# Head rounds: every eviction of a projection unit placed ahead of the attention work of its slot on ScalarE

## The chip, the cores and the metric

One Trainium2 chip, one core. The metric is the device time in microseconds of one execution of the whole layer; the numbers given for a kernel are its median over several executions. Profiled times come from one further execution, taken by the hardware profiler.

## The reference, cut to what matters

One decoder layer on x of 1 x 1024 x 1024, all in float32:

```python
proj = rms_norm(x) @ w_in            # q, k, v of 8 attention heads; q, k, v, i, f, o of 8 mLSTM heads; gates
oa = diff_attention(q, k, v)         # per head: softmax(q0 k0) - lam * softmax(q1 k1), causal, times v
hm = mlstm_chunkwise(qm, km, vm, i, f)
ya, yb = rms(oa) @ w_proj_a, (sigmoid(ml_o) * rms(hm)) @ w_proj_b
h = x + (g0 * ya + g1 * yb) @ w_out
h = h + relu(rms_norm(h) @ w_ff1) ** 2 @ w_ff2
out = rms_norm(h)
```

## The kernel before

Everything is written by hand: each engine has its own instruction stream, and semaphores order the streams.

The input projection is cut into blocks of 128 output columns, and each block into two halves of 512 positions. One half is a *unit*: 24 matmuls of 128x512 (three split products for each of 8 slices of the contraction, L716 to L718) into one of two PSUM banks, `gp[0]` for even units and `gp[1]` for odd ones. A head needs 6 blocks, so 12 units, numbered 0 to 11. ScalarE evicts a unit with `evac` (L1059 to L1064): it waits until the *previous* contents of the SBUF buffer `ev[0]` or `ev[1]` are stored (`st`), then until the matmuls are done, copies 128x512 (L1062) and signals SyncE, which stores the buffer to DRAM (`proj_d`, L400). TensorE may start unit k+2 only when unit k is evicted.

The projection of head h runs interleaved with the attention of head h-1. This is a *head round*: rounds 1 to 7 are run by `head_round(h, h - 1)` on each engine. A round has 16 slots. The table `QUARTERS` says how many quarter units TensorE computes in each slot, (4, 4, 5, 0, 3, 2, 3, 3, 4, 4, 4, 4, 2, 2, 4, 0), and `ENDS_AT[s]` lists the units that end in slot s. No slot ends more than one: units 0, 1 and 2 end in slots 0, 1 and 2, unit 3 in slot 4, units 4 to 9 in slots 6 to 11, units 10 and 11 in slots 13 and 14. In each slot TensorE first does its quarters and then `attend(att, s)`, the attention work.

The slots that matter below, on ScalarE (`attend`, L1157):

- Slot 0: it copies the rotated k four times (`ka`, `kb`, L1166 to L1170), then q twice (L1166, L1167), then v (`vs`, L1161).
- Slot 2: it copies the transposed mLSTM v (`v1`, shown as `v` at L1178, done when TensorE has transposed it, L785), and loads the Exp table with a small activation (`warm`, L1180).
- Slots 3 to 10: the softmax exponentials of query block s-3 (`pr`, L1207), two passes. VectorE makes from them the combined attention row (`at`, L1611), which TensorE transposes in the next slot, after its quarters (L871); ScalarE copies the transposed row (`ath`, L1186), VectorE makes its low part (`atl`, L1583), and only behind that, in VectorE's order, come the maxima of the next block's scores.
- Slots 5 and 6: additionally four exponentials of 128x128 each over a row that is broadcast from DRAM (`qraw` from `u_d`, L1215).
- Slots 5 to 12: a copy of the accumulated output (`otmp`, L1195) ahead of the `ath` copy.

SyncE issues its DMAs in a written order, one queue. At the start of a round it issues: the stores of the last round's units, the loads of the attention's k, q and v, a weight block, `ckq` and `osig` (512 KB each, L438 and L440), the store of unit 0, the store of unit 1, a weight block, the two broadcast rows (L449), the store of unit 2, the store of unit 3, and so on.

In ScalarE's `head_round` the eviction of a slot's unit stands behind the slot's attention work; in slot 0 it stands between the four k copies and the two q copies. The gate round that follows round 7 has its own loop with the same form.

Of the kernel before, what the change touches and what calls it, by code (L numbers as in the profile page):

```python
# [44 lines left out]
HB = 6  # L45
# [38 lines left out]
def part_slots(quarters):  # L84

    at = [s for s, n in enumerate(quarters) for _ in range(n)]
    starts = [[k for k in range(2 * HB) if at[4 * k] == s] for s in range(SLOTS)]
    ends = [[k for k in range(2 * HB) if at[4 * k + 3] == s] for s in range(SLOTS)]
    return at, starts, ends


QUARTER_AT, STARTS_AT, ENDS_AT = part_slots(QUARTERS)
# [6 lines left out]
def wait(eng, sem, value):  # L99

    if isinstance(value, int) and value <= 0:
        return
    eng.wait_ge(sem, value)
# [27 lines left out]
def build(nc, x, positions, norm_mix_w, w_in, ml_gate_b, conv_w, conv_b, da_lambda, da_subln_w,  # L131
# [14 lines left out]
    with ExitStack() as ctx:  # L146
# [905 lines left out]
        def _(act):  # L1052
# [6 lines left out]
            def evac(n, half):  # L1059
                wait(act, st[half], 16 * n)  # L1060
                act.wait_ge(gemm_done, 2 * n + half + 1)
                act.activation(ev[half][:], gp[half][:], ACT.Copy).then_inc(gp_free, 1)  # L1062
                act.wait_ge(gp_free, 2 * n + half + 1)
                act.sem_inc(ev_ready[half], 1)  # L1064
# [76 lines left out]
            def units_of_round(h, k):  # L1141
                if k % 2 == 0:
                    b = k // 2
                    split_hi(h * HB + b + 1, h * (HB // 2) + (b + 1) // 2, (b + 1) % 2)

            def kq_wait(h, b):
                if b + 1 == 3:
                    act.wait_ge(w_loaded_q, 16 * h + 16)
# [99 lines left out]
            def head_round(h, att):  # L1248
                for s in range(SLOTS):
                    for k in STARTS_AT[s]:  # L1250
                        if k % 2 == 0:
                            kq_wait(h, k // 2)
                            units_of_round(h, k)
                    for k in ENDS_AT[s][:-1]:
                        evac(h * HB + k // 2, k % 2)

                    def evac_units():
                        for k in ENDS_AT[s][-1:]:
                            evac(h * HB + k // 2, k % 2)

                    attend(att, s, evac_units)
                    if s:
                        evac_units()

            head_round(1, 0)
            with act.Fori(2, NH) as h:
                head_round(h, h - 1)
# [27 lines left out]
            for j in range(2 * KT):  # L1295
# [7 lines left out]
                else:  # L1303
                    for i in range(2):
                        k = j - KT
# [800 lines left out]
```

## Time and profile before

| | |
|---|---|
| median of 3 runs | 2007.83 us (2005.05 to 2009.06) |
| profiled execution: time, span | 2009.17 us, 2007.4 us |
| TensorE busy | 96% of the span |
| VectorE, ScalarE, GpSimd busy | 59%, 48%, 18% |
| rounds 1 to 7 | about 130 to 870 us of the span |
| evictions L1062 in the whole kernel | 128, 591 ns each |
| stores of evictions | 128, 256 KB each |

Rows of the profile give the start in us from the start of the span, the duration in us, then engine, line and operation with output and inputs. A bracket at the end holds the idle time of the engine just before it and what ended it. For a DMA the landing time is the time from its issue until all its data are there.

### The profile page before, as it was taken

The numbers are of one execution on the slowest core, as the hardware profiler recorded it, in microseconds if no ns is written. First come the engines' busy times: TensorE is split into PE (matmuls) and PEld (weight loads), VectorE is DVE, ScalarE is ACT, GpSimd is POOL, SyncE is SP. The second block draws the span as 40 slices with busy tenths as digits, with TensorE's granted clock in tenths as the row PEclk, the third lists the DMA queues.
The fourth block names the chain that finished last, engine by engine and source line by source line (L and its number), as shares of the span: only waits on it lengthen the run. The fifth ranks groups of instructions, "written<-read, shape, count | busy, mean of one in ns | idle before, by whom it ended". The sixth has DMA issues, their size and how long they took to land. (4 is left out here: it accounts for less than half of the span.)

```text
span 2007.4 us, 26057 instructions
## 1 busy us (share of the span) xinstructions
PE 1923.8 (96%) x9378; PEld 1605.9 (80%) x9378; DVE 1180.8 (59%) x1537; ACT 966.1 (48%) x1634; POOL 364.8 (18%) x204
## 2 busy tenths in 40 slices
PE   5989999999999999999998999999999999999998
PEld 4768888788888787878886888888888888888886
DVE  5736666566575757543321112278677787888874
ACT  4346565556465555544433333225765765533341
POOL 1211211212111121211121444441000000021002
PEclk9989999999999999999999999999999999999999
DMA  5562657645544546273435443645686785563422
GB/s 150 88 153 66 148 84 131 99 120 107 123 104 110 120 72 158 59 176 70 68 88 162 155 150 104 224 157 210 220 289 210 255 281 196 210 237 132 163 82 84
DMA packets 207825, 291.79 MB, mean 145 GB/s; under 512 B 36840, under 2 KB 127592, under 8 KB 200832
## 3 DMA queue, kind: packets, MB, share of 16 engines
q1 hardware_dynamic: 195520, 281.98, 50.9%
q10 hardware_dynamic: 12224, 8.72, 1.3%
q8 instruction: 52, 0.85, 0.2%
q14 instruction: 29, 0.24, 0.0%
HBM read 203.56 MB, written 87.10 MB: 145 GB/s over the span
## 5 line engine op out<-in xcount | busy, mean ns | idle before, releaser
L716 PE MATMUL gp<-r1h,w_hi 128*128 128x512 f32 x1152 | 457.4, 397 | 13.9 <-ACT ev L1062 12.3
L718 PE MATMUL gp<-r1h,w_lo 128*128 128x512 f32 x1152 | 452.1, 392 | 0.0
L717 PE MATMUL gp<-r1l,w_hi 128*128 128x512 f32 x1152 | 451.6, 392 | 0.0
L1967 POOL TENSOR_TENSOR w_lo<-w_raw,w_hi 128x1024 fp32r<-128x1024 f32 x88 | 219.2, 2491 | 896.8 <-ACT w_hi L1057 896.8
L716 PEld LDWEIGHTS gp<-r1h,w_hi 128*128 128x128 f32 x1152 | 218.2, 189 | 59.7 <-issue 8.1
L718 PEld LDWEIGHTS gp<-r1h,w_lo 128*128 128x128 f32 x1152 | 217.8, 189 | 46.6
L717 PEld LDWEIGHTS gp<-r1l,w_hi 128*128 128x128 f32 x1152 | 218.3, 189 | 42.3
L977 PE MATMUL scores<-xh,qh 128*128 128x512 f32 x512 | 200.1, 391 | 1.4 <-ACT res L1367 1.3
L981 PE MATMUL scores<-xh,ql 128*128 128x512 f32 x512 | 199.3, 389 | 0.0
L979 PE MATMUL scores<-xl,qh 128*128 128x512 f32 x512 | 199.2, 389 | 0.0
L1207 ACT ACTIVATE pr<-scores,nb 128x256 f32<-128x256 f32 (+7 forms) x128 | 93.9, 739 | 122.2 <-DVE nb L1601 120.6
L1779 DVE TENSOR_TENSOR xl<-xraw,xh 128x2048 fp32r<-128x2048 f32 x54 | 127.8, 2367 | 0.0
L1062 ACT ACTIVATE ev<-gp 128x512 f32<-128x512 f32 x128 | 75.6, 591 | 87.9 <-PE gp L718 49.4
L1321 ACT ACTIVATE qh<-rq 128x2048 fp32r<-128x2048 f32 x32 | 61.2, 1914 | 114.8 <-DVE rq L1808 73.8
L1057 ACT ACTIVATE w_hi<-w_raw 128x1024 fp32r<-128x1024 f32 x88 | 93.2, 1059 | 47.8 <-PE gp L718 20.4
L977 PEld LDWEIGHTS scores<-xh,qh 128*128 128x128 f32 x512 | 96.1, 188 | 23.5 <-ACT res L1367 3.0
L1599 DVE TENSOR_REDUCE mx<-scores 128x1 f32<-128x256 f32 (+7 forms) x128 | 91.4, 750 | 38.6 <-PE scores L811 38.1
L981 PEld LDWEIGHTS scores<-xh,ql 128*128 128x128 f32 x512 | 96.1, 188 | 20.1
L979 PEld LDWEIGHTS scores<-xl,qh 128*128 128x128 f32 x512 | 96.1, 188 | 20.0 <-issue 0.2
L1333 ACT ACTIVATE xh<-xraw 128x2048 fp32r<-128x2048 f32 x54 | 102.8, 1904 | 9.2 <-DMA xraw<-xo_d 9.2
L716 PE MATMUL gp<-r2h,w_hi 128*128 128x512 f32 x256 | 102.1, 399 | 3.5 <-issue 3.5
L1783 DVE TENSOR_TENSOR ql<-rq,qh 128x2048 fp32r<-128x2048 f32 x32 | 76.6, 2392 | 46.4 <-ACT qh L1321 46.4
(340 smaller groups left out, 3650.8 us busy)
## 6 DMA issues: line engine op xcount, KB each, us to landing
xraw<-xo_d SPq DMA_DIRECT2D x54, 1024.0 KB, 5.1
proj_d<-ev SPq DMA_DIRECT2D x128, 256.0 KB, 3.2
rq<-in_w_ff SPq DMA_DIRECT2D x32, 1024.0 KB, 7.8
w_raw<-in_w_in SPq DMA_DIRECT2D x56, 512.0 KB, 9.2
xo_d<-res SPq DMA_DIRECT2D x78, 256.0 KB, 3.2
xo_d<-ring SPq DMA_DIRECT2D x60, 256.0 KB, 2.9
pr<-proj_d SPq DMA_DIRECT2D x16, 512.0 KB, 5.6
gt<-proj_d SPq DMA_DIRECT2D x32, 256.0 KB, 2.7
```

Source lines behind the costliest of these rows:

```text
L716: pe.matmul(gp[half][:], wh[slot][:, k, :], mh[:, k, t], start=(k == 0), stop=False)
L717: pe.matmul(gp[half][:], wh[slot][:, k, :], ml[:, k, t], start=False, stop=False)
L718: mm = pe.matmul(gp[half][:], wl[slot][:, k, :], mh[:, k, t], start=False, stop=(k == KT - 1))
L977: pe.matmul(bank, qh[s % 3][:, k, cols], xh[s % 3][:, k, :], start=first and k == 0, stop=False, skip_group_check=True)
L979: pe.matmul(bank, qh[s % 3][:, k, cols], xl[s % 3][:, k, :], start=False, stop=False, skip_group_check=True)
L981: mm = pe.matmul(bank, ql[s % 3][:, k, cols], xh[s % 3][:, k, :], start=False, stop=(k == UN - 1), skip_group_check=True)
L1057: act.activation(wh[slot][:], raw[slot][:], ACT.Copy).then_inc(w_hi, 1)
L1207: act.activation(pr[:, c, 0:(i + 1) * P], sp_[:, c, 0:(i + 1) * P], ACT.Exp, bias=nb[:, c:c + 1], scale=SCALE, accum_out=rs[:, i, c:c + 1] ...
L1333: act.activation(xh[s % 3][:], xraw[(s + 1) % 2][:], ACT.Copy).then_inc(p_hi, 1)
L1599: m = dve.tensor_reduce(mx[:, c:c + 1], sp_[:, c, 0:(i + 1) * P], AX_X, ALU.max)
L1779: dve.tensor_tensor(xl[s % 3][:], xraw[(s + 1) % 2][:], xh[s % 3][:].bitcast(F32), ALU.subtract).then_inc(p_lo, 1)
L1967: pool.tensor_tensor(wl[slot][:], raw[slot][:], wh[slot][:].bitcast(F32), ALU.subtract).then_inc(w_split, 1)
```

## The change

The eviction of the unit that ends in a slot is moved, on ScalarE, from behind `attend(att, s)` to in front of it, in all slots of rounds 1 to 7. In slot 0 it moves from between the k copies and the q copies to ahead of the k copies. Nothing is added or removed; no other engine's stream is edited, and the gate round keeps its form.

```diff
-                    for k in ENDS_AT[s][:-1]:
+                    for k in ENDS_AT[s]:
                         evac(h * HB + k // 2, k % 2)
-
-                    def evac_units():
-                        for k in ENDS_AT[s][-1:]:
-                            evac(h * HB + k // 2, k % 2)
-
-                    attend(att, s, evac_units)
-                    if s:
-                        evac_units()
+                    attend(att, s, lambda: None)
```

## Rows read from the trace of the kernel before

**Rows 1.** Waits of TensorE, 140 to 1000 us: what waited, total us, times, longest

```profile
PE tr L871 <- DVE at L1611: 7.2, 3, 2.8
PE gp L716 <- ACT ev L1062: 6.9, 3, 3.5
PE tr L905 <- DVE nd L1682: 6.2, 7, 0.9
```

**Rows 2.** Timeline of ScalarE in round 5, slots 0 to 4

```profile
554.12 1.06 ACT L1166 ACTIVATE ka<-kraw 64x1024 fp32r<-64x1024 f32 x1 [3.66 <-DVE kraw L1570]
...
558.34 0.58 ACT L1062 ACTIVATE ev<-gp 128x512 f32<-128x512 f32 x1
...
567.29 0.60 ACT L1178 ACTIVATE v<-tr 128x512 f32<-128x512 f32 x1 [1.93 <-PE tr L785]
...
568.40 1.28 ACT L1180 ACT_TABLE_LOAD   x1
...
569.80 0.58 ACT L1062 ACTIVATE ev<-gp 128x512 f32<-128x512 f32 x1
570.63 0.37 ACT L1207 ACTIVATE pr<-scores,nb 128x128 f32<-128x128 f32 x1 [0.25 <-ACT ev L1062]
...
572.83 0.28 ACT L1186 ACTIVATE ath<-tr 128x128 fp32r<-128x128 f32 x1 [1.39 <-PE tr L871]
```

**Rows 3.** Timeline of TensorE in round 5: attention work of slots 2, 4, 5

```profile
566.60 0.66 PE L785 MATMUL tr<-ident,pr 128*128 128x128 f32 x4 [0.51 <-DVE vs L1578]
...
572.46 0.33 PE L871 MATMUL tr<-ident,at 128*128 128x128 f32 x1
...
576.57 0.44 PE L871 MATMUL tr<-ident,at 128*128 128x128 f32 x2
```

**Rows 4.** Timeline of VectorE in round 5, slot 4

```profile
576.03 0.48 DVE L1611 SCALAR_TENSOR_TENSOR at<-pr,cc 128x256 f32<-128x256 f32 x1
```

**Rows 5.** Timeline of SyncE in round 5: issue, us that it took

```profile
556.76 0.34 SPq L440 DMA_DIRECT2D osig<-proj_d  x1
559.12 1.48 SPq L400 DMA_DIRECT2D proj_d<-ev  x1
```

**Rows 6.** Landing of these two DMAs, last column, us from issue

```profile
osig<-proj_d SPq DMA_DIRECT2D x1, 512.0 KB, 10.0
proj_d<-ev SPq DMA_DIRECT2D x1, 256.0 KB, 8.3
```

**Rows 7.** Round 6: timeline of ScalarE, slots 2 and 3

```profile
676.40 0.60 ACT L1062 ACTIVATE ev<-gp 128x512 f32<-128x512 f32 x1 [2.11 <-DMA proj_d<-ev]
677.25 0.37 ACT L1207 ACTIVATE pr<-scores,nb 128x128 f32<-128x128 f32 x1 [0.25 <-ACT ev L1062]
```

**Rows 8.** Round 6: timeline of TensorE, slot 4

```profile
679.08 0.33 PE L871 MATMUL tr<-ident,at 128*128 128x128 f32 x1 [2.16 <-DVE at L1611]
```

**Rows 9.** Round 2: issues of SyncE

```profile
240.54 1.67 SPq L440 DMA_DIRECT2D osig<-proj_d  x1
242.40 2.14 SPq L400 DMA_DIRECT2D proj_d<-ev  x1
```

**Rows 10.** Round 2: eviction of unit 2, ScalarE

```profile
251.24 0.58 ACT L1062 ACTIVATE ev<-gp 128x512 f32<-128x512 f32 x1
```

**Rows 11.** Round 3: ScalarE in slot 5, exponentials over the broadcast row

```profile
371.74 1.29 ACT L1215 ACTIVATE qraw<-qraw,hk 128x128 f32<-128x128 f32 x4 [3.91 <-DMA qraw<-u_d]
```

**Rows 12.** Round 3: issues of the stores of units 2 and 3, SyncE

```profile
358.88 6.92 SPq L400 DMA_DIRECT2D proj_d<-ev  x2
```

**Rows 13.** Round 3: landing of the first of them

```profile
proj_d<-ev SPq DMA_DIRECT2D x1, 256.0 KB, 14.8
```

**Rows 14.** Round 4: ScalarE in slot 5, exponentials over the broadcast row

```profile
477.75 1.29 ACT L1215 ACTIVATE qraw<-qraw,hk 128x128 f32<-128x128 f32 x4 [1.20 <-DMA qraw<-u_d]
```

**Rows 15.** Round 4: issue of the store of unit 2, SyncE

```profile
466.84 3.56 SPq L400 DMA_DIRECT2D proj_d<-ev  x1
```

**Rows 16.** Round 4: landing of that store

```profile
proj_d<-ev SPq DMA_DIRECT2D x1, 256.0 KB, 12.8
```

## Prediction

> **What bounds the kernel now.** TensorE is busy for 96% of the span, so a change on ScalarE counts only where TensorE waits for what ScalarE delivers. I read the waits of TensorE over the head rounds first, then the timelines of ScalarE, TensorE, VectorE and SyncE through slots 0 to 7, then the landing times of the stores. The waits [rows 1] show two things. Waiting for an eviction (`gp` for `ev`) costs 6.9 us in three places; all three lie after 890 us, in the gate round, whose code stays as it is. In rounds 1 to 7 TensorE never waits over 0.25 us for an eviction, so there is nothing to win by evicting earlier. What it does wait for is the attention chain: `tr` for `at` 7.2 us in three places, in rounds 3, 6 and 7, and `tr` for `nd` 0.9 us in each of seven rounds.
>
> The chain has no slack in slots 2 to 4. In round 5 ScalarE copies v at 567.29, loads the Exp table, evicts unit 2 at 569.80 and starts the first exponential at 570.63 [rows 2]. VectorE's row and TensorE's transposition of it follow; that starts at 572.46, 1.83 after the exponential, just as the quarters of slot 4 run out [rows 3]. Round 6 shows what a delay does: there the eviction of unit 2 waits 2.11 us for DMA, namely for the store of unit 0 that used the same buffer; the exponential starts at 677.25 [rows 7], the transposition at 679.08, again 1.83 later, and TensorE has waited 2.16 us [rows 8]. A late exponential is paid by TensorE one for one.
>
> **The change part by part.** 128x512 evictions stay 84 in number in these rounds, at 0.58 to 0.61 us. Only their order to other work changes, so each is priced by what it now stands before.
>
> *Slots 0 and 1.* Unit 0 ends at about 553, and ScalarE then idles until the rotated k at 554.12, with 3.66 us of idle before it [rows 2]: the eviction fits there, free. Behind the k copies it was free too, since the q copies wait for VectorE. Unit 1 has no attention work in its slot. Cost 0. If k came before the unit's end, up to 0.6 would be paid, but I see no such round.
>
> *Slot 2, the term that decides.* The eviction of unit 2 now stands before the v copies, the table load and the first exponential. Its wait for the store of unit 0 moves along. Before, a late store was covered by 2.5 us of copies and table load (567.29 to 569.80) [rows 2]. Now this work is queued behind the wait. After the store lands, the chain is: eviction 0.6, hand-over 0.2 to 0.3, then from the start of the v copies to the end of `warm` 2.6, so the exponential starts 3.4 to 3.5 after landing; before, it started 0.85 after landing, or at 570.63 if that was later.
>
> Does the store land earlier? The eviction of unit 0 ends some 5 us earlier, but SyncE issues the store behind `osig`, at 559.12 now, and is free only at 557.1 [rows 5]. `osig` lands at 556.76 + 10.0 = 566.8, the store at 559.12 + 8.3 = 567.4 [rows 5, 6], that is 0.6 behind it: it waits for the data queued before. I take the same landing; the other bound is 2 us earlier in round 5. In round 2 SyncE is busy with `osig` until 242.2 and stores at 242.40 [rows 9], so there is no earlier issue at all; its store also takes 8.3 (one row stands for both, [rows 6]) and lands at 250.7.
>
> The Trainium skill (DMA: Bandwidth & Descriptors, Queues, rings and completion order) states that on each DMA engine descriptors are consumed in ring order. The landings of `osig` and the store, 0.6 apart where the issues are 2.4 apart, agree with it; by it the earlier issue gains nothing.
>
> With these landings, round by round for the first exponential:
> - Round 5: eviction 567.4, exponential about 570.8 to 570.9 for 570.63: +0.2.
> - Round 2: 250.7 + 3.45 = 254.15. Before, the eviction was at 251.24 [rows 10] and the exponential 0.84 behind it: +2.1.
> - Round 6: landing 676.35, exponential 679.85 for 677.25 [rows 7]: +2.5. Round 7 repeats this pattern (one of the three waits of [rows 1]): +2.5.
> - Rounds 1 and 4: the store is there before unit 2 is done; the exponential comes 0.7 earlier, which gains nothing since TensorE had no wait there.
> - Round 3: about +2.4 here, but see slot 6.
>
> *Slot 4.* The eviction of unit 3, done when the quarters of slot 4 end, comes before the copy of the transposed row (`ath`, 572.83 [rows 2]). ScalarE is free at that point, so the eviction starts about 572.6 and the copy about 573.4: +0.5. Behind it in VectorE's order are the low part and the maxima of block 1; the row of block 1 (`at`, 576.03 + 0.48 [rows 4]) ends just before TensorE transposes it at 576.57 [rows 3]. So +0.5 in rounds where slot 2 brought no delay (1, 4, 5); where it did, the eviction runs while ScalarE waits, cost 0. Bounds: 0 (if the copy is covered) to 0.8 in all seven.
>
> *Slot 6.* The eviction of unit 4 comes before the output copy and the `ath` copy of block 2. By itself it costs about 0.1 at the next transposition. But it waits for the store of unit 2, which SyncE issues behind the broadcast rows. In round 3: issue 358.88, landing 14.8, so 373.7 [rows 12, 13], while ScalarE was done with the exponentials of slot 5 at 371.74 + 1.29 = 373.0, having waited 3.91 for the broadcast row [rows 11]. So the copies move from 372.9 to 374.5: +1.6. The broadcast row lands at a time set by DMA, so the +2.4 of slot 2 is swallowed by that 3.91 us wait: round 3 in all +1.6. In round 4: landing 466.84 + 12.8 = 479.6 [rows 15, 16] against 477.75 + 1.29 = 479.0 [rows 14]: +1.3, which contains its 0.5 of slot 4. In the other rounds the store is there.
>
> *Slots 7 to 14.* From slot 7 to 11 ScalarE runs behind TensorE, each slot ends one unit, and between two attention parts there stands one eviction before and after the change; cost 0. In slots 13 and 14 it waits for TensorE and VectorE anyway; the 0.9 us for `nd` [rows 1] stay. If that cover is gone, one eviction a round would be paid, 7 x 0.6 = 4.2.
>
> Sum: round 1 0.5, round 2 2.1, round 3 1.6, round 4 1.3, round 5 0.6 (0.2 + 0.5, rounded down), rounds 6 and 7 2.5 each: 11.1 us. The profiled execution took 2009.17, so 2020.3. It is 1.3 above the median of the runs shown; that gives 2019.
>
> **Rivals.**
>
> *Nothing measurable.* The stores land soon enough that no eviction waits. For it: each round's late landing is chance of the moment, and in round 5 it is a matter of tenths. Then the two waits of rounds 6 and 7 go too (-2.2 each), and slot 4 costs 0.5 in seven rounds: -0.9, so 2007. The Trainium skill (DMA: Bandwidth & Descriptors, Anatomy of one DMA) fits a DMA as about 2.0 us plus bytes over 436 GB/s, given for the GpSimd path; for 256 KB that is an estimate of 2.6 us and would give this rival. Against it: 8.3 to 14.8 measured here for exactly these stores.
>
> *Faster.* The store of unit 0, evicted 5 us earlier, gets ahead in the DMA queues, lands over 4 us sooner, so that the waits of rounds 6 and 7 vanish (-4.4), and slot 4 is covered: the 0.7 us earlier first exponential gives VectorE its convolution step earlier. 2007.8 - 4.4 = 2003.4. It decides from a landing before the v transposition ends (567.25 in round 5). Against it: SyncE's written order and the wait behind `osig`.
>
> *Slower by half.* The store lands by as much earlier as it is issued earlier (2 us in round 5, 1 in rounds 6 and 7), and the slot-4 and slot-6 costs are partly covered: rounds 6 and 7 1.5 each, round 2 2.1, rounds 3 and 4 1 each: about 7, 2014.5.
>
> *Much slower.* The eviction also holds up slots 7 to 11, and each round stalls once more: 11.1 + 4.2, 2023.
>
> **How the numbers follow.** Chances: forecast 0.40, slower by half 0.22, much slower 0.12, nothing measurable 0.16, faster 0.10. A change under 0.2%, 4 us, can't be told from none here. Of the "slower by half" and forecast cases a part of 0.02 falls within 4 us. So slower 0.72, same 0.18, faster 0.10. Range: from the no-change case, 2006.5, to a little over "much slower", 2024.
>
> **What would show it.** In the profile of the changed kernel, evictions L1062 with a DMA store as releaser in several of rounds 2 to 7, ahead of the v copies, and the table load L1180 behind them; TensorE's `tr` for `at` wait growing from 7.2 us to some 16 us or more, in slots 4, 5 and 7; the `gp` wait of the gate round and the `nd` waits unchanged. If no eviction of unit 2 waits for DMA, the slot-2 term is wrong; if the transposition of block 1 still follows the quarters without a gap in round 1, the slot-4 term is.

## The result

The changed kernel took 2022.53 us in the median of seven runs (2014.54 to 2023.92), against 2005.05 (2003.02 to 2009.06) for the kernel before: a ratio of 1.0074 with a 95% interval of 1.0059 to 1.0089, so 12 to 18 us slower, about 15; the two medians themselves lie 17.5 apart. 11 were forecast. What a kernel is "over" or "under" the kernel before is worked out from such a ratio here and in the experiments, and can differ by up to 3 us from the distance of the medians. One execution of one experiment (e6) ran at a mean granted clock of 0.85 in place of 0.99 and took 2144.18 us; it is left out. The profiled execution took 2019.78 us, with a span of 2018.0, 10.6 more than before.

Every engine executes the same instructions. What grew is TensorE's waiting. The page of the changed kernel has it busy for 1921.5 us of a longer span, where it was 1923.8 of 2007.4 before:

```profile
PE 1921.5 (95%) x9378; PEld 1606.4 (80%) x9378; DVE 1175.0 (58%) x1537; ACT 965.4 (48%) x1634; POOL 370.8 (18%) x204
```

The waits of TensorE in the changed kernel, 140 to 1000 us, columns as in [rows 1]:

```profile
PE tr L871 <- DVE at L1604: 17.1, 9, 4.7
PE gp L716 <- ACT ev L1062: 9.2, 4, 3.8
PE tr L905 <- DVE nd L1675: 6.2, 7, 1.1
PE ob L857 <- DVE atl L1576: 5.7, 8, 1.1
```

Against [rows 1], the wait of the transposition for the attention row has gone from 7.2 us in three places to 17.1 in nine; for an eviction from 6.9 to 9.2, of which 2.05 are new in round 3 and the rest lies behind round 7 as before. The wait for `nd` is still 6.2.

ScalarE in round 6 of the changed kernel, to be read beside [rows 7]. The eviction of unit 2 stands first and waits 6.73 us for DMA; the v copy, the table load and the first exponential come behind it:

```profile
685.14 0.60 ACT L1062 ACTIVATE ev<-gp 128x512 f32<-128x512 f32 x1 [6.73 <-DMA proj_d<-ev]
685.92 0.60 ACT L1178 ACTIVATE v<-tr 128x512 f32<-128x512 f32 x1 [0.18 <-ACT ev L1062]
...
687.02 1.28 ACT L1180 ACT_TABLE_LOAD   x1
...
688.43 0.35 ACT L1207 ACTIVATE pr<-scores,nb 128x128 f32<-128x128 f32 x1
```

TensorE in the same round; the wait was 2.16 us in [rows 8]:

```profile
690.24 0.47 PE L871 MATMUL tr<-ident,at 128*128 128x128 f32 x1 [4.66 <-DVE at L1604]
```

The store that it waits for, SyncE's timeline and then the landing times. It is issued right behind `osig` and lands at 671.20 + 13.8 = 685.0, as `osig` does within 0.7 us (670.67 + 13.7 = 684.4):

```profile
670.67 0.34 SPq L440 DMA_DIRECT2D osig<-proj_d  x1
671.20 5.31 SPq L400 DMA_DIRECT2D proj_d<-ev  x1
```

```profile
osig<-proj_d SPq DMA_DIRECT2D x1, 512.0 KB, 13.7
proj_d<-ev SPq DMA_DIRECT2D x1, 256.0 KB, 13.8
```

How far the changed kernel has fallen behind is read from one landmark in each round, the start of the transposition of `nd` in slot 15 (L905), which both timelines show; what each round adds stands beside the forecast:

| round | before, us | after, us | behind by | added in the round | forecast |
|---|---|---|---|---|---|
| 1 | 227.75 | 229.15 | 1.4 | 1.4 | 0.5 |
| 2 | 332.18 | 335.24 | 3.1 | 1.7 | 2.1 |
| 3 | 441.58 | 448.86 | 7.3 | 4.2 | 1.6 |
| 4 | 546.29 | 554.86 | 8.6 | 1.3 | 1.3 |
| 5 | 650.68 | 659.36 | 8.7 | 0.1 | 0.6 |
| 6 | 757.28 | 770.36 | 13.1 | 4.4 | 2.5 |
| 7 | 863.98 | 878.09 | 14.1 | 1.0 | 2.5 |

After round 7 the changed kernel, in this one profiled execution, gains 3.5 us back, in code that is the same in both. That part varies from run to run and is not laid to the change.

Round 6 adds 1.9 us more than the slot-2 term. The windows of TensorE in the changed kernel (start and end, length, busy, granted clock, DMA share, GB/s) show why:

```profile
688.00:690.00 2.00, 0.00 (x0) 0.79 0.67 242
690.00:692.00 2.00, 1.76 (x8) 0.50 0.61 235
692.00:694.00 2.00, 2.00 (x6) 0.50 0.19 76
694.00:696.00 2.00, 2.00 (x6) 0.50 0.05 18
696.00:698.00 2.00, 2.00 (x14) 1.00 0.00 0
```

During the wait of 4.66 us the granted clock falls from 1.00 to 0.50, from the 2.4 to the 1.2 GHz level, and stays there for some 6 us of matmuls, with 6 matmuls in 2 us where there are 14 in the last row (128x512 ones among smaller ones). In the kernel before, the wait of 2.16 us in this round brought no fall; that of 2.82 us in round 3 did, as does the one of 3.20 us in the same place of the changed kernel. So a wait can cost its length and then some.

Round 3 has a term that was forecast at nothing. The eviction of unit 0, in slot 0 and now ahead of the k copies, waited 6.06 us for the last round's store, and everything behind it on ScalarE moved back with it, the eviction of unit 1 too, for which TensorE later had to wait. ScalarE's timeline, then TensorE's:

```profile
345.52 0.60 ACT L1062 ACTIVATE ev<-gp 128x512 f32<-128x512 f32 x1 [6.06 <-DMA proj_d<-ev]
346.33 1.06 ACT L1166 ACTIVATE ka<-kraw 64x1024 fp32r<-64x1024 f32 x1 [0.21 <-ACT ev L1062]
```

```profile
356.05 0.50 PE L716 MATMUL gp<-r1h,w_hi 128*128 128x512 f32 x1 [2.05 <-ACT ev L1062]
```

What it cost is seen further on. SyncE may load the next weight block only when the last one in that buffer is split (`w_split`, set by GpSimd behind ScalarE's copy `w_hi`, which itself follows the eviction of unit 1), and it issues the broadcast row behind that load. SyncE's timeline before, then of the changed kernel:

```profile
354.49 0.44 SPq L449 DMA_DIRECT2D qraw<-u_d  x1
```

```profile
360.56 0.44 SPq L449 DMA_DIRECT2D qraw<-u_d  x1
```

The issue comes 6.1 us later, 3.0 more than the 3.1 by which the changed kernel was behind at the end of round 2. The row takes as long to land as before (17.1 us, 17.2 before), and slot 5, where ScalarE waits for it (3.91 us before, 4.00 now), comes later by as much. The other runs agree. Taking off what each kernel was behind at the end of round 2, the issue in round 3 comes 2.9 us later in e2, 2.8 in e7 and 3.5 in e8, which have slot 0 ahead and two buffers, but 0.1 in e1, where slot 0 is as before, and 0.0 in e3, where no store is waited for.

### The profile page after: what moved, and what is told of

It is laid out like the page before. It is cut to its first block and busy times, and to the rows that moved or that the text cites. A ratio compares the mean times of both kernels' runs of the same rounds, so it can differ in the third digit from the quotient of the medians.

```text
span 2018.0 us, 26057 instructions
## 1 busy us (share of the span) xinstructions
PE 1921.5 (95%) x9378; PEld 1606.4 (80%) x9378; DVE 1175.0 (58%) x1537; ACT 965.4 (48%) x1634; POOL 370.8 (18%) x204
## 5 line engine op out<-in xcount | busy, mean ns | idle before, releaser
L1960 POOL TENSOR_TENSOR w_lo<-w_raw,w_hi 128x1024 fp32r<-128x1024 f32 x88 | 225.6, 2564 | 903.5 <-ACT w_hi L1057 903.5
```

The costliest lines, as they stand in the source:

```text
L1960: pool.tensor_tensor(wl[slot][:], raw[slot][:], wh[slot][:].bitcast(F32), ALU.subtract).then_inc(w_split, 1)
```

## The experiments

Theory A: the price is the wait for an earlier store, which now stands in front of the attention work, chiefly in slot 2, and 0.7 us a round in slot 4. Theory B: it is 0.6 us of eviction ahead of each slot's attention, spread over all slots. The experiments e1 to e4 ran on one chip, e5 to e8 on a second and e9 and e10 on a third, each group with the kernel before beside it, whose medians were 2007.25, 2004.96 and 2005.21 us.

### One slot's order at a time, two buffers

Both kernels use this form in place of the changed lines, with (2,) and with all slots but 2:

```diff
-                    for k in ENDS_AT[s]:
+                    for k in ENDS_AT[s] if s in AHEAD else ():
                         evac(h * HB + k // 2, k % 2)
-                    attend(att, s, lambda: None)
+
+                    def evac_units():
+                        for k in () if s in AHEAD else ENDS_AT[s]:
+                            evac(h * HB + k // 2, k % 2)
+
+                    attend(att, s, evac_units)
+                    if s:
+                        evac_units()
```

> Only the eviction of unit 2 (slot 2) stands ahead of the attention work; in all other slots it stays behind, as before. Theory A (the price is the wait for the store of unit 0, with the v copies, the table load and the first exponential queued behind it): most of the loss is here, 9 to 12 us over before, and TensorE waits 1.9 to 4.7 us for the first row in slot 4 of rounds 2, 6 and 7. Theory B (the loss comes from 0.6 us of eviction ahead of every slot's attention, spread evenly): at most 3 us over before.

Measured: 2015.57 us, ratio 1.0047 (1.0032 to 1.0063), 9.4 over before. TensorE's waits in rounds 1 to 7:

```profile
PE tr L873 <- DVE at L1613: 13.7, 4, 4.8
```

Four waits for the first row, 1.96, 2.48, 4.38 and 4.84 us, in rounds 2, 3, 6 and 7. The wait of 2.82 us that the kernel before has in slot 7 of round 3 is not among them: the delay in slot 4 of that round took its place, so that the round adds nothing (landmark 3.0 us behind before, 3.6 at the end of round 2). One slot of sixteen carries more than half of the loss, as theory A has it. The granted clock fell to 0.50 behind all four, where before it fell behind one wait in these rounds.

> The change in every slot but slot 2, whose eviction stays behind its attention work. Theory A: 3 to 6 us over before (slot 4 with 0.7 us in each round, slot 6 in rounds 3 and 4), and no eviction of unit 2 in front of the v copies. Theory B: 12 to 14 us over before.

Measured: 2013.07 us, ratio 1.0030 (1.0019 to 1.0040), 6 over before: the upper end of theory A, half of theory B. The two parts, 9.4 and 6, add up to the whole change's 15. The waits for the attention row:

```profile
PE tr L873 <- DVE at L1613: 12.1, 10, 3.2
PE gp L718 <- ACT ev L1064: 2.1, 1, 2.1
```

Three of the ten, 2.1 to 3.2 us, are the three of the kernel before. New are five in slot 5 of rounds 1 to 5, 0.49 to 0.69 us, which are the forecast's slot 4, and two in slot 7, 0.45 in round 2 and 1.14 in round 4, its slot 6. The second row is the slot-0 term of round 3 again, with ScalarE's eviction waiting 5.98 us for the store.

### Four buffers: the store wait taken away

Evicted units rotate through four SBUF buffers with a semaphore each, so an eviction waits for the store of two blocks ago. The cut shows `evac` alone; `p` is the parity of the block, and `before` counts the stores of this buffer so far:

```diff
-                wait(act, st[half], 16 * n)
+                wait(act, st[p][half], 16 * before)
                 act.wait_ge(gemm_done, 2 * n + half + 1)
-                act.activation(ev[half][:], gp[half][:], ACT.Copy).then_inc(gp_free, 1)
+                act.activation(evs[p][half][:], gp[half][:], ACT.Copy).then_inc(gp_free, 1)
```

> The changed kernel with four SBUF buffers for evicted units in place of two, so that an eviction waits for the store of two blocks ago and not of the last one. Theory A: no eviction in rounds 1 to 7 waits for DMA; slot 4 keeps its 0.7 us a round; the time falls from the changed kernel's by 12 us or more, to within 5 us of before on either side. Theory B, or if the order alone is to blame: it stays 10 us or more over before.

Measured: 1994.52 us, ratio 0.9942 (0.9929 to 0.9955). With the order of the change and no store waits the kernel is 28 us faster than the changed one, and 12 faster than before, which is beyond the band that I gave. No eviction waits for DMA. The waits that are left in rounds 1 to 7:

```profile
PE tr L879 <- DVE at L1619: 8.5, 9, 3.2
```

One of them, in round 4, TensorE's timeline; the same wait, 0.69 to 0.72 us, stands in slot 5 of all seven rounds, and none in before ([rows 3], 576.57):

```profile
474.23 0.44 PE L879 MATMUL tr<-ident,at 128*128 128x128 f32 x2 [0.71 <-DVE at L1619]
```

> The kernel before with the same four buffers. Theory A: the waits of 2.1 us in slot 2 of rounds 6 and 7 vanish (4.4 us), and with them those of 8.2 and 6.5 us of ScalarE in the gate round and behind it, for which TensorE paid 3.5 us each: 6 to 13 us faster than before. Rival: the stores are no limit once one wait moves to the next DMA (the broadcast row): no change within 3 us.

Measured: 1989.35 us (1988.60 to 1992.16), ratio 0.9917 (0.9904 to 0.9931): the fastest kernel of this study, 33 us under the changed one and 17 under before, more than expected. In rounds 1 to 7 one wait for the attention row is left of three:

```profile
PE tr L877 <- DVE at L1617: 2.9, 1, 2.9
```

Only 3.8 us are gained there (slot 15 of round 7 starts at 860.17 for 863.98). The larger part lies behind round 7: the wait of 3.50 us for an eviction at 891 us is gone, and with it about 7 us at a reduced clock. So is a stall of 3.52 us at 1097 us, where ScalarE's eviction had waited 6.53 us for a store. Three other waits of TensorE for an eviction in the gate round, 1.5, 1.9 and 1.5 us, stay with four buffers (1.48, 1.91 and 1.49), and so does one of 3.5 (3.61): the store is not their cause. Windows of TensorE in the kernel before, then in this one:

```profile
890.00:892.00 2.00, 0.73 (x2) 0.61 0.81 150
892.00:894.00 2.00, 2.00 (x7) 0.50 0.70 140
894.00:896.00 2.00, 2.00 (x6) 0.50 0.73 165
896.00:898.00 2.00, 2.00 (x7) 0.68 0.73 206
```

```profile
892.00:896.00 4.00, 4.00 (x21) 1.00 0.83 258
```

This pair gives the order's own price where no store is waited for: 1994.52 - 1989.35 = 5.2 us. In the two profiled executions, whose spans differ by 5.0 us, only 2.2 of it are there at slot 15 of round 7 (862.35 for 860.17); the rest arises later, in code that is the same in both, and no run says whether the order causes it.

### Which slots make up the 5.2 us

All with four buffers, in the form of the first two experiments.

> Four buffers, and only the eviction of unit 3 (slot 4) ahead of its slot's attention work. Theory A: what is left of the change without DMA waits is slot 4 alone, so the whole 5 us between the two four-buffer kernels comes back: 4.5 to 5.5 us over the order of before with four buffers (1989.4), with TensorE waiting 0.7 us for the second row in each of seven rounds. Rival (all slots share it): 1 us or less.

Measured: 1991.26 us, 1.9 over 1989.35. The seven waits are there, one of 0.72 and six of 0.47 to 0.52 us, 3.7 us in all, but the median is less than expected. The profiled execution, at 1995.44 us the slowest of its six, would fit the expectation (at slot 15 of round 7 it is 4.6 us behind e4), but it also has the clock at 0.50 for about 7 us in round 3, where e4 has it for about 4.

> Four buffers, every eviction ahead but the one of slot 4. Theory A: within 1 us of 1989.4. Rival: 3 to 5 us over it.

Measured: 1991.16 us, 1.8 over, between the theory's span and the rival's (the median with the execution at the low clock is 1992.15); no wait in slot 5 is left. The two complements add up to 3.7 of 5.2. My theory that slot 4 alone is left fell: a new wait of 1.18 us stands in slot 7 of round 4. I formed two others: slot 6, or slots 7 to 14.

> Four buffers, only the eviction of unit 4 (slot 6) ahead of its slot's attention work. Theory C (the rest of the 5 us, beyond slot 4, is slot 6: where the broadcast row lands late, ScalarE's output copy now stands behind row, exponentials and eviction): 0.5 to 2 us over the order of before with four buffers (1989.4), with a new TensorE wait of about 1 us for the row of block 3 in round 4. Theory D (it is slots 7 to 14): within 0.5 us of 1989.4.

Measured: 1994.95 us, 5.6 over, well beyond the 0.5 to 2 of theory C. Two new waits, 0.42 in round 2 and this one in round 4 (TensorE's timeline):

```profile
490.80 0.44 PE L879 MATMUL tr<-ident,at 128*128 128x128 f32 x2 [1.43 <-DVE at L1619]
```

Behind it, ScalarE in this kernel waits 1.76 us for the broadcast row, and then the eviction goes ahead of the output copy:

```profile
483.38 1.28 ACT L1223 ACTIVATE qraw<-qraw,hk 128x128 f32<-128x128 f32 x4 [1.76 <-DMA qraw<-u_d]
484.57 0.58 ACT L1070 ACTIVATE ev<-gp 128x512 f32<-128x512 f32 x1
485.32 0.28 ACT L1203 ACTIVATE otmp<-ob 128x128 f32<-128x128 f32 x1 [0.17 <-ACT ev L1070]
```

Of the 1.43 us, 0.75 are the eviction; about 0.5 more is the row, which in e4 lands that much earlier against the rest of the round (ScalarE waits 1.23 us for it there).

From slot 15 of round 1 to that of round 7 this kernel takes 634.17 us for 631.65, so 2.5 us are slot 6's. The profile also shows 2.6 us before the first edited instruction works: the first attention transposition starts at 131.95 for 129.35. Whether that belongs to the edit is open; a kernel that differs in slot 6 alone should not differ there. The clock is down for 3 us longer at that point than in e4.

> Four buffers, the evictions of slots 7 to 14 ahead, those of slots 0 to 6 behind. Theory C: within 1 us of 1989.4, since between two attention parts there stands one eviction either way; TensorE's wait of 0.55 us for the low part in slot 10 stays what it is. Theory D: 2 to 3 us over it.

Measured: 1990.26 us, 0.9 over, and 631.38 us between the same two landmarks, 0.3 less. By the trace slots 7 to 14 are free, so theory C holds for the place. The sizes don't come out: 1.9 for slot 4, 0.9 for slots 7 to 14 and 5.6 for slot 6 are more than 5.2 together. Nor can they, since e5 to e10 ran on other chips than e4, and a difference of a microsecond or two can't be resolved between them. Three measures of the same kernels, each less that of e4:

| | median, us | by the ratio to the kernel before of the same chip, us | slot 15 of round 1 to that of round 7, profiled, us |
|---|---|---|---|
| e3, all slots | 5.2 | 5.0 | 2.0 |
| e5, slot 4 | 1.9 | 2.8 | 3.9 |
| e6, all but slot 4 | 1.8 | 2.6 | 1.0 |
| e9, slot 6 | 5.6 | 6.0 | 2.5 |
| e10, slots 7 to 14 | 0.9 | 2.4 | -0.3 |

The ratios have intervals of 2 to 3 us to either side, so by the times alone theory D, which put e10 at 2 to 3 us, is not excluded. Against it stands the trace: no wait for the attention row is new in slots 8 to 15.

### The store of unit 0 earlier in the queue

Two buffers; SyncE issues the store of unit 0 ahead of the loads of `ckq` and `osig` (and no longer in its old place, a line that the cut leaves out):

```diff
                         if b == 1:
+                            store(h * HB, (0,))
                             ml_loads(att)
```

> The changed kernel, two buffers, with one edit on SyncE: the store of unit 0's buffer is issued ahead of the loads of ckq and osig, not behind them. Theory A with a queue (the store lands late because it stands behind 1 MB of loads): it lands 3 to 8 us after its issue and before unit 2 is done, the slot-2 waits vanish and the time falls by 9 to 13 us from the changed kernel's, to 2007 to 2012; slot 4 and slot 6 stay. Rival (DMA is simply slow at this point of a round, wherever the store stands): no more than 3 us gained.

Measured: 2008.22 us, ratio 1.0015 (1.0004 to 1.0027): 12 to 14 us back from the changed kernel, as expected. But the way there was not. In round 6 the store, issued at 666.25, lands 13.3 us later, not 3 to 8; the eviction of unit 2 still waits, 2.45 us in place of 6.73 (in round 7 2.28 for 5.68). TensorE's wait in slot 4 shrinks all the same, from 4.66 to 0.36. ScalarE's timeline:

```profile
679.64 0.60 ACT L1065 ACTIVATE ev<-gp 128x512 f32<-128x512 f32 x1 [2.45 <-DMA proj_d<-ev]
```

Right ahead of it stand two loads of 256 KB, the halves of a weight block, in pieces of 256 bytes (64 columns of 4 bytes). The first, issued at 665.03, lands after 6.2 us; the second, issued by 665.7, after 13.3, so at about 679, next to the store's 666.25 + 13.3 = 679.55. Counted from the issue of the first half, the store lands after 14.5 us here and after 18.8 in the changed kernel (666.25 to 685.0). So `ckq` and `osig` are some 4 us of its lateness, and the rest was there without them. That the rest is the weight block's is read from the common landing alone; no run puts the store ahead of it.

> Two buffers, the order of before, but the eviction of unit 0 ahead (slot 0 alone) and its store issued ahead of ckq and osig. Theory A with a queue: the waits of 2.1 us in slot 2 of rounds 6 and 7 vanish, nothing is added: 3 to 6 us faster than before. Rival: ckq and osig land later and the convolution of slot 3 with them, no gain.

Measured: 2002.57 us, ratio 0.9986 (0.9977 to 0.9994), 2 to 3 us faster than before, just under the 3 to 6 expected. The waits of 2.16 and 2.20 us of rounds 6 and 7 are gone. In round 3 the eviction in slot 0 waits 6.55 us for the last round's store, TensorE then waits 1.59 us for the eviction of unit 1, and the round takes 3.0 us more than before. So the early eviction in slot 0 could be turned to use together with the store's new place; what either would do alone was not run.

## Why the prediction was right

**Slot 2** was right in place, kind and, where the clock kept still, in size. In round 6 of the changed kernel the exponential starts 688.43 - 685.0 = 3.4 us behind the landing, as worked out, and the transposition 1.81 behind that. TensorE's wait grew from 2.16 to 4.66, by 2.5, the forecast value, because the landing was rightly taken as that of the queue: an eviction 5 us earlier brought nothing. In rounds 2, 5 and 7 the waits are 1.91, 0.36 and 3.60 us, which is 1.9, 0.4 and 1.4 more, for 2.1, 0.2 and 2.5. What was missing is the clock: the long wait of round 6 lowered it and cost 1.9 us on top. In e1 it fell in each of the four rounds, and slot 2 alone cost 9.4 us there where the waits of rounds 2, 6 and 7 had been put at 7.1; TensorE's waits for the row grew by 6.5 us in that trace, and the falls are the likely rest.

**Slot 4** was put at 0.5 us in three rounds. It is 0.7 in every round in which slot 2 brings no delay (e3: 0.69 to 0.72), and about 0.5 where the eviction of unit 2 stays behind (e5). It was put right in kind: the eviction, then `ath`, then VectorE's low part, then the maxima. What it is worth in the time is not settled: 1.9 us by e5's median, where 3.7 us of waits are seen, and 3.9 us between the landmarks of its trace.

**Slot 6** was named for rounds 3 and 4, and both came as forecast. In round 3 of the changed kernel the exponentials over the broadcast row end at 377.69 + 1.28 = 378.97, the eviction waits 0.76 us for the store, and the copies start at 380.50, so 1.6 later than they would, the forecast value. Round 4 cost 1.3 us in all, with the eviction waiting 0.76 us for the store behind 0.66 for the broadcast row (ScalarE's and TensorE's timelines of the changed kernel):

```profile
484.95 1.28 ACT L1215 ACTIVATE qraw<-qraw,hk 128x128 f32<-128x128 f32 x4 [0.66 <-DMA qraw<-u_d]
486.99 0.60 ACT L1062 ACTIVATE ev<-gp 128x512 f32<-128x512 f32 x1 [0.76 <-DMA proj_d<-ev]
```

```profile
493.24 0.66 PE L871 MATMUL tr<-ident,at 128*128 128x128 f32 x4 [1.22 <-DVE at L1604]
```

The forecast's "by itself it costs about 0.1" was too low: e9 shows a wait of 1.43 us in round 4 with no store wait at all. Where the broadcast row is late the eviction adds its full 0.75 to a chain without slack; the other half is a later row.

**Slot 0** was said to be free; this is the step that failed. The wait for the last round's store was overlooked there: 6.06 us in round 3 of the changed kernel (14.97 in round 1, where TensorE waited 9.64 us for DMA itself and the round adds 1.4 in all), and 4.2 us added in that round where 1.6 were forecast. It is not the wait of 2.05 us for unit 1 that makes the round longer, but the broadcast row, issued 3.0 us late: TensorE's transposition in slot 7 starts 7.6 us later than before (385.98 for 378.38), which is the 3.1 that the kernel was behind already, these 3.0 and slot 6's 1.6, within 0.1. The same holds in e2 (round 3 adds 4.1) and, without slot 6, in e8 (3.0). With round 6's 1.9 for the clock this 2.6 is the larger part of what the forecast of 11 lacked; round 1 added 0.9 more than forecast, and rounds 5 and 7 gave 2.0 back. So the sum over the rounds, 14.1 for 11.1, is near the forecast in part because terms too low and too high offset each other.

**Slots 7 to 14** were put at nothing, and e10's trace shows that: 631.38 us from slot 15 of round 1 to that of round 7, for 631.65. The rival by which they stall each round had the time that comes nearest, 2023 for the measured median of 2022.5, but not the cause: it needs 0.6 us a round in these slots, and what is seen there is 0.1, by which TensorE's wait for the low part in slot 10 grows (0.5 to 0.6 us before, 0.6 to 0.7 in e10 and in the changed kernel).

**That nothing is to be won**, since TensorE waits for no eviction in rounds 1 to 7, was right; the evictions that it does wait for lie behind round 7. For the one of 3.50 us at 891 e4 shows that the cause is the store, not the place.

The rival in which the store lands in time is excluded by the 29.2 us that ScalarE's evictions waited for DMA in nine places between 140 and 880 us, 4.3 in two before. The faster rival needed the store of unit 0 to get ahead of the queue; in the changed kernel it did not, and e7 shows that in round 6 it lands 13.3 us after its issue even with its own place ahead of `ckq` and `osig`.

## What to carry to other kernels

An eviction has two waits, for the matmuls and for the store that last used its buffer; before it is moved ahead of other work on an in-order engine, look up where that store lands, for whatever now stands behind it inherits the wait. Where a store stands behind large loads in one queue, its landing time is that of the queue, and a second pair of buffers (4 KB a partition here) was worth more than any order that was tried: 17 us of 2005. A wait that TensorE does not feel at once can still move what a later slot depends on, as the eviction of slot 0 moved the broadcast row. And read which evictions TensorE waits for before reordering any: here none lay in the part that was changed.

## What was not expected of the hardware

TensorE's granted clock fell from 1.00 to 0.50 behind some waits and cost more than the wait: in the changed kernel behind 4.66 us of idle in round 6, for about 6 us of matmuls. It did not follow the length of the wait alone. It also fell behind 1.96 us of idle in round 2 of e1 and behind 2.82 us in round 3 of the kernel before, and it stayed at 1.00 behind 2.16 and 2.20 us in the latter's rounds 6 and 7 and behind the 3.60 us in round 7 of the changed kernel:

```profile
800.19 0.33 PE L871 MATMUL tr<-ident,at 128*128 128x128 f32 x1 [3.60 <-DVE at L1604]
```

In both of the changed kernel's rounds TensorE had been busy for 3.4 to 4.0 us of every 4 in the 20 us (round 6) and 16 us (round 7) ahead of the wait; what decides is open.
